# Three of eight k pairs of each gate/up block by Strassen's seven products

## The reference, cut to what matters

```
hn = rms_norm(h, ffn_norm[i])
h = h + (jax.nn.silu(hn @ w_gate[i]) * (hn @ w_up[i])) @ w_down[i]
```

## Time and profile before

| | us |
|---|---|
| median of 3 runs | 1336.36 (1336.12 to 1336.68) |
| profiled execution, its own time | 1335.7 |
| its span, first to last instruction | 1333.8 |
| PE busy in the span | 1327.3 (100%) |
| DVE busy | 789.4 (59%) |
| ACT busy | 629.2 (47%) |

### The profile page before, as it was taken

The page is one execution under the profiler, slowest core; times in us unless marked ns, Lnnn a source line. Parts: engine busy times, 40 slices in busy tenths (PEclk is TensorE's granted clock), DMA queues, the critical chain, the costliest instruction groups (busy, mean ns, idle before and its releaser), DMA issues.

```text
span 1333.8 us, 18088 instructions
## 1 busy us (share of the span) xinstructions
PE 1327.3 (100%) x6718; PEld 1097.8 (82%) x6718; DVE 789.4 (59%) x987; ACT 629.2 (47%) x796; POOL 54.2 (4%) x71
## 2 busy tenths in 40 slices
PE   9999999999999999999999999999999999999998
PEld 7788888887888888888888888888888888888887
DVE  6578885788585555555555554444555555555554
ACT  6576444543555545444444443344444444444543
POOL 4002000320000000000000000000000000000000
PEclk9999999999999999999999999999999999999999
DMA  8555544554445566666666666666666666655564
GB/s 270 172 182 164 152 143 135 158 155 136 136 128 156 176 190 189 190 194 185 188 188 194 186 189 196 196 190 192 186 189 192 189 186 190 189 188 190 189 191 141
DMA packets 126200, 238.34 MB, mean 179 GB/s; under 512 B 9711, under 2 KB 10786, under 8 KB 126138
## 3 DMA queue, kind: packets, MB, share of 16 engines
q1 hardware_dynamic: 126106, 237.48, 59.0%
q10 hardware_dynamic: 32, 0.01, 0.0%
HBM read 235.36 MB, written 2.10 MB: 178 GB/s over the span
## 4 chain that ended last, share of the span: by engine, by line
PE 99%; DMA 0%; DVE 0%; ACT 0%; issue 0%; ACTq 0%
PE pair L559 30%; PE pair L561 30%; PE pair L560 30%; PE bg L678 2%; PE bg L748 2%; PE bg L615 1%; PE bg L833 1%; PE bg L729 0%; PE bg L592 0%; PE pair L903 0%; PE pair L901 0%; PE pair L902 0%; PE bg L643 0%; PE bg L650 0%; PE bg L659 0%; DMA row_a<-in_attn_norm_dram 0%
## 5 line engine op out<-in xcount | busy, mean ns | idle before, releaser
L1233 DVE TENSOR_TENSOR w_lo<-raw,w_hi 128x1024 fp32r<-128x1024 f32 x442 | 540.3, 1225 | 420.4 <-ACT w_hi L919 417.5
L919 ACT ACTIVATE w_hi<-raw 128x1024 fp32r<-128x1024 f32 x442 | 467.8, 1061 | 485.0 <-PE pair L561 481.9
L559 PE MATMUL pair<-w_hi,xT_hi 128*128 128x512 f32 x1264 | 502.5, 398 | 0.5 <-DVE w_lo L1457 0.5
L561 PE MATMUL pair<-w_hi,xT_lo 128*128 128x512 f32 x1264 | 493.1, 390 | 0.0
L560 PE MATMUL pair<-w_lo,xT_hi 128*128 128x512 f32 x1264 | 492.5, 390 | 0.0
L561 PEld LDWEIGHTS pair<-w_hi,xT_lo 128*128 128x128 f32 x1264 | 237.2, 188 | 50.5
L559 PEld LDWEIGHTS pair<-w_hi,xT_hi 128*128 128x128 f32 x1264 | 237.4, 188 | 48.3 <-issue 0.7
L560 PEld LDWEIGHTS pair<-w_lo,xT_hi 128*128 128x128 f32 x1264 | 237.6, 188 | 46.0
L559 PE MATMUL pair<-w_hi,actT_hi 128*128 128x512 f32 x352 | 137.7, 391 | 0.0
L561 PE MATMUL pair<-w_hi,actT_lo 128*128 128x512 f32 x352 | 137.1, 389 | 0.0
L560 PE MATMUL pair<-w_lo,actT_hi 128*128 128x512 f32 x352 | 137.0, 389 | 0.0
(11 more groups left out here) (234 smaller groups left out, 875.4 us busy)
## 6 DMA issues: line engine op xcount, KB each, us to landing
raw<-in_w_in_dram SPq DMA_DIRECT2D x112, 512.0 KB, 3.8
raw<-in_w_gate_dram SPq DMA_DIRECT2D x88, 512.0 KB, 4.5
raw<-in_w_up_dram SPq DMA_DIRECT2D x88, 512.0 KB, 3.8
raw<-in_w_down_dram SPq DMA_DIRECT2D x88, 512.0 KB, 4.6
raw<-in_w_o_dram SPq DMA_DIRECT2D x32, 512.0 KB, 4.2
raw<-in_w_ple_gate_dram SPq DMA_DIRECT2D x32, 512.0 KB, 4.4
raw<-in_w_ple_proj_dram SPq DMA_DIRECT2D x4, 512.0 KB, 4.5
h<-in_x_dram SPq DMA_DIRECT2D x3, 512.0 KB, 7.7
```

What stands on the lines that cost most here:

```text
L559: mm(banks[t][:], hi[:, ts], wh, start=first, stop=False)
L561: m = mm(banks[t][:], lo[:, ts], wh, start=False, stop=last)
L919: f(w_hi[j % RING][:], raw[j % RING][:], ACT.Copy).then_inc(hi_ready, 1)
L1233: v.tensor_tensor(w_lo[j % RING][:], raw[j % RING][:], w_hi[j % RING][:].bitcast(F32), ALU.subtract).then_inc(lo_ready, 1)
```

## The change

In k pairs 3, 4 and 5 (`MIXED`) of every block, the gate unit and the up unit of the pair are used together. The pair's product is a 2 x 2 block product: tokens in two halves (0 and 1) by two k tiles (0 and 1), times two k tiles by (gate, up). It is made with Strassen's seven products (the Winograd form) instead of eight, 21 matmuls instead of 24.

- The differences of weights are made by DVE: t3, t1 (in place, over the up unit's first tile), t2 and t4, each from the one before or from raw tiles; ACT rounds them, DVE makes their low parts (`split_mixed`). Their buffers `t_hi`, `t_lo` are single and are free when PE has used them (`t_used`).
- The sums and differences of activations (`F_raw`, `F_hi`, `F_lo`) are made once, in steps hA 3, 4 and 5. For the other five pairs (`PLAIN`) hA also makes the difference of the two token halves (`d_hi`, `d_lo`), since the second up bank now gathers a product with this difference.
- The units come in the order `SEQ`: gate 0, 1, 2, 6; gate and up 3; gate 7; gate and up 4; up 0; gate and up 5; up 1, 2, 6, 7.
- The pair products go to `bg[0]`, `bg[1]`, `bg[2]` and the four `pair` banks. Sums bring them together: four on DVE for the gate after the third pair (`MIXED_END`), with one copy on ACT, and three for up at the end of the block.
- PE turns `act_s` behind unit 2 instead of unit 3, and waits for `ff_free` before the first mixed pair. Steps hA 6 and 7 come one unit earlier. SP's fetch into a mixed gate unit's tile waits for `t4_ready`.

```diff
-            at[U_WO + (n + 1) * UPB + 2][g].append(("hA", 2 * n + g))
+            at[U_WO + (n + 1) * UPB + (2 if n < 3 else 1)][g].append(("hA", 2 * n + g))
...
+MIXED = (3, 4, 5)
+PLAIN = [g for g in range(UPB) if g not in MIXED]
+SEQ = ([("gate", g) for g in PLAIN[:4]] + [("gate", MIXED[0]), ("up", MIXED[0])] + [("gate", g) for g in PLAIN[4:]]
+       + [("gate", MIXED[1]), ("up", MIXED[1])] + [("up", PLAIN[0])]
+       + [("gate", MIXED[2]), ("up", MIXED[2])] + [("up", g) for g in PLAIN[1:]])
+MIXED_END = SEQ.index(("up", MIXED[-1]))
...
+                        if j >= RING and SEQ[j - RING] in [("gate", m) for m in MIXED]:
+                            sp.wait_ge(t4_ready, i * len(MIXED) + (len(MIXED) * at + MIXED.index(SEQ[j - RING][1]) + 1))
+                            fetch(j, w, KU * g, i * CB + at * CB)
+                        else:
+                            load(i * (2 * UPB) + (u0 + j), j, w, KU * g, i * CB + at * CB)
...
+            def product(o, hi, lo, wh, wl, first, last):
+                mm(o, hi, wh, start=first, stop=False)
+                mm(o, hi, wl, start=False, stop=False)
+                return mm(o, lo, wh, start=False, stop=last)
+            def mixed_units(u, j, q, n):
...
+                use(u)
+                product(bg[0][:], xT_hi[:, k0, a0], xT_lo[:, k0, a0], gh[:, 0, :], gl[:, 0, :], first, last)
+                product(pair[0][0][:], xT_hi[:, k1, a0], xT_lo[:, k1, a0], gh[:, 1, :], gl[:, 1, :], False,
+                        last).then_inc(unit_used, 1)
+                use(u + 1)
+                product(pair[1][1][:], xT_hi[:, k0, a1], xT_lo[:, k0, a1], uh[:, 0, :], ul[:, 0, :], first, False)
+                product(pair[1][0][:], F_hi[:, q, 1, :], F_lo[:, q, 1, :], uh[:, 1, :], ul[:, 1, :], first,
+                        False).then_inc(unit_used, 1)
+                pe.wait_ge(t3_lo_ready, n)
+                product(bg[2][:], F_hi[:, q, 2, :], F_lo[:, q, 2, :], t_hi[:, 2, :], t_lo[:, 2, :], first, last)
+                pe.wait_ge(t24_lo_ready, n)
+                product(bg[1][:], F_hi[:, q, 0, :], F_lo[:, q, 0, :], t_hi[:, 0, :], t_lo[:, 0, :], first, last)
+                product(pair[0][1][:], xT_hi[:, k1, a1], xT_lo[:, k1, a1], t_hi[:, 1, :], t_lo[:, 1, :], False,
+                        last).then_inc(t_used, 1)
...
+                        if q == 0:
+                            pe.wait_ge(pair_free[1], i * 2 + b0)
+                            if not peeled:
+                                for n in range(2):
+                                    pe.wait_ge(ff_free[n], i + n0)
+                        mixed_units(u, j, q, i * len(MIXED) + (len(MIXED) * n0 + q + 1))
...
-                    if j == 3 and not peeled:
+                    if j == 2 and not peeled:
                         pe.wait_ge(pair_free[1], i * 2 + b0)
+                        pe.wait_ge(gate_sum, i * 2 + 2 * n0)
                         turn_act()
...
+            def split_mixed(u, j, n, n0_first):
+                act.wait_ge(t3_ready, n)
+                if not n0_first:
+                    act.wait_ge(t_used, n - 1)
+                f(t_hi[:, 2, :], t3_raw[:], ACT.Copy).then_inc(t3_hi_ready, 1)
+                act.wait_ge(t1_ready, n)
+                act.wait_ge(unit_used, u - (RING - 1))
+                f(w_hi[j % RING][:], raw[j % RING][:], ACT.Copy).then_inc(hi_ready, 1)
+                act.wait_ge(t4_ready, n)
+                f(t_hi[:, 0:2, :], t24_raw[:], ACT.Copy).then_inc(t24_hi_ready, 1)
...
+            def split_mixed(u, j, n, first):
+                jg, ju = (j - 1) % RING, j % RING
...
+                v.tensor_tensor(t3_raw[:], raw[ju][:, 1, :], raw[ju][:, 0, :], ALU.subtract).then_inc(t3_ready, 1)
+                dve.wait_ge(t3_ready, n)
+                v.tensor_tensor(raw[ju][:, 0, :], raw[ju][:, 0, :], raw[jg][:, 0, :], ALU.subtract).then_inc(t1_ready, 1)
+                dve.wait_ge(t1_ready, n)
+                v.tensor_tensor(t24_raw[:, 0, :], raw[ju][:, 1, :], raw[ju][:, 0, :], ALU.subtract).then_inc(t2_ready, 1)
+                dve.wait_ge(t2_ready, n)
+                v.tensor_tensor(t24_raw[:, 1, :], raw[jg][:, 1, :], t24_raw[:, 0, :], ALU.subtract).then_inc(t4_ready, 1)
+                split(u, j)
+                dve.wait_ge(t3_hi_ready, n)
+                v.tensor_tensor(t_lo[:, 2, :], t3_raw[:], t_hi[:, 2, :].bitcast(F32), ALU.subtract).then_inc(t3_lo_ready, 1)
+                dve.wait_ge(t24_hi_ready, n)
+                v.tensor_tensor(t_lo[:, 0:2, :], t24_raw[:], t_hi[:, 0:2, :].bitcast(F32),
+                                ALU.subtract).then_inc(t24_lo_ready, 1)
...
+                    if j == MIXED_END:
+                        p1 = act_s[1]
+                        dve.wait_ge(p1_copied, i + (n0 + 1))
+                        v.tensor_tensor(v_s[:], bg[1][:], p1[:], ALU.add).then_inc(v_ready, 1)
+                        v.tensor_tensor(gate_s[0][:], pair[0][0][:], p1[:], ALU.add).then_inc(gate_sum, 1)
+                        dve.wait_ge(v_ready, i * 2 + (2 * n0 + 1))
+                        v.tensor_tensor(u_s[:], bg[2][:], v_s[:], ALU.add).then_inc(v_ready, 1)
+                        dve.wait_ge(v_ready, i * 2 + (2 * n0 + 2))
+                        v.tensor_tensor(gate_s[1][:], pair[0][1][:], u_s[:], ALU.add).then_inc(gate_sum, 1)
...
+                        v.tensor_tensor(v_s[:], pair[1][1][:], v_s[:], ALU.add).then_inc(up_sum, 1)
+                        v.tensor_tensor(u_s[:], pair[1][1][:], u_s[:], ALU.add).then_inc(up_sum, 1)
+                        dve.wait_ge(up_sum, i * 3 + (3 * n0 + 1))
+                        v.tensor_tensor(v_s[:], pair[1][0][:], v_s[:], ALU.add).then_inc(up_sum, 1)
```

More of the change, by code:

```diff
@@ L251, in build @@
         ident = sb("ident", [P, P])
+        triu_at = place[0]
+        t24_raw = sb("t24_raw", [P, 2, CB], at=triu_at)
         triu = sb("triu", [P, P])
@@ L259, in build @@
         NROW = 3 * KT + 3
+        assert triu_at + 4 * KIB <= place[0]
         rows = sb("rows", [NROW - KT, P])
@@ new lines, in mixed_units @@
+            def mixed_units(u, j, q, n):
+                first, last = q == 0, q == len(MIXED) - 1
+                g, a0, a1 = MIXED[q], slice(0, P), slice(P, TOK)
+                k0, k1 = KU * g, KU * g + 1
+                gh, gl = w_hi[j % RING], w_lo[j % RING]
+                uh, ul = w_hi[(j + 1) % RING], w_lo[(j + 1) % RING]
+                use(u)
[12 more added lines that the diff above has]
+                        last).then_inc(t_used, 1)
@@ new lines, in gate_up @@
+            def gate_up(i, u0, b0, n0, peeled):
+                for j, (side, g) in enumerate(SEQ):
+                    u = i * (2 * UPB) + (u0 + j)
+                    if g in MIXED:
+                        if side == "up":
+                            continue
+                        q = MIXED.index(g)
+                        if q == 0:
[4 more added lines that the diff above has]
+                        mixed_units(u, j, q, i * len(MIXED) + (len(MIXED) * n0 + q + 1))
+                        continue
+                    use(u)
+                    if j == 0:
+                        pe.wait_ge(pair_free[0], i * 2 + b0)
+                    if peeled and n0 == 0 and g in (PLAIN[0], 6) and side == "gate":
+                        for n in (range(6) if g == PLAIN[0] else (6, 7)):
+                            wait_read(pe, ("hA", n))
+                    for kk in range(KU):
+                        k = KU * g + kk
+                        wh, wl = w_hi[j % RING][:, kk, :], w_lo[j % RING][:, kk, :]
+                        if side == "gate":
+                            last = k_tile(j, kk, xT_hi[:, k, :], xT_lo[:, k, :], pair[0], k == 0, False)
+                        else:
+                            d = KU * PLAIN.index(g) + kk
+                            product(pair[1][1][:], xT_hi[:, k, P:TOK], xT_lo[:, k, P:TOK], wh, wl, False, k == KT - 1)
+                            last = product(pair[1][0][:], d_hi[:, d, :], d_lo[:, d, :], wh, wl, False, k == KT - 1)
@@ L947, in post @@
                         act.wait_ge(x1_full, 1)
+                    if step == "hA" and b in MIXED:
+                        if b - 1 in MIXED:
+                            wait_read(act, (step, b - 1))
+                        for kk in range(2):
+                            k = 2 * b + kk
+                            f(xg[:, kk, :], bk[:, kk * TOK:(kk + 1) * TOK], ACT.Copy,
+                              scale=gains[:, col + k:col + k + 1]).then_inc(xg_ready, 1)
+                        q = MIXED.index(b)
+                        act.wait_ge(xg_ready, 2 * (q + 1))
+                        f(xT_hi[:, 2 * b, 0:P], xg[:, 0, 0:P], ACT.Copy)
+                        f(xT_hi[:, 2 * b + 1, :], xg[:, 1, :], ACT.Copy).then_inc(x_hi, 2)
+                        act.wait_ge(form_ready, 4 * q + 1)
+                        f(xT_hi[:, 2 * b, P:TOK], F_raw[:, 0, :], ACT.Copy)
+                        act.wait_ge(form_ready, 4 * (q + 1))
```

(45 more changed lines are left out.)

89 lines of the change are left out of this document (67 added, 22 removed).

## The result

| | us |
|---|---|
| before, median of 6 runs | 1336.43 |
| changed kernel, median of 6 runs | 1343.95 (1341.92 to 1347.19) |
| ratio, 95% interval | 1.0057 (1.0044 to 1.0070) |
| profiled execution's span | 1341.3 (before 1333.8) |
| mean granted clock in it | 0.995 (before 0.999) |

The kernel is slower by 0.6%, 7.5 us, though PE got 99 matmuls fewer. The runs spread over 5 us where those of before spread over 0.6.

A forecast was written before the change was run, and what follows sets the result against it. PE was taken to bound the kernel, busy all the time with 99% of the chain. Saved matmuls -22.4, waits for the turned banks +21.3 and the first block +2.75 gave +1.65 us: 1338.0 us, range 1331.5 to 1346.

The forecast's parts named there:

- the three signs: Whole kernel: chances of 0.24 for faster by over 0.2%, 0.35 for within 0.2%, 0.41 for slower.
- its own band: Whole kernel: 1334 to 1343 us, from a wait of 2.1 to 2.8 us per block; chance 0.52.
- further waits in each block: Behind `turned`, margins of 0.3 to 0.5 us fail: 0.6 us per block in ten blocks, 1344 us; chance 0.20.
- 99 matmuls at 0.2267: -22.4: Mixed pairs on PE: 99 fewer matmuls at 0.2267 us each save 22.4 us, 2.04 per block.
- The wait for the turned banks, nine times 2.37: Before the first mixed pair, PE waits for DVE to free the turned banks: nine blocks, 21.3 us.
- T+13.91: DVE's `turned` operations end 13.91 us after T, the first matmul of a block; PE wants them at T+11.76.
- The first block: 2.75: First gate/up block: PE loses 1.55 us at unit 3 for hA, some 0.6 at each later pair.
- The rest of the block at nothing: Behind the first pair's wait, thin cover suffices: 0 us taken, bounds 0 to 1 us per block.
- The clock: Behind PE's idle times, the clock falls to 1.2 GHz, half a us nine times: +4.5, 1342.6 us; chance 0.05.
- The rival that own waits cost nothing: In DVE's chain, waits on its own results are free, shortening each PE wait to 1.89 us: 1332.2; chance 0.12.
- The rival that DVE keeps ahead: At the turned banks, DVE frees them in time, leaving only the first block's 2.75 us loss: 1316.7; chance 0.11.

The follow-up runs named there:

- own_bank: Changed kernel with the pairs' first product in the unused bank bg[3] and the ff_free wait moved before the product into bg[1]: 1316.17 us, ratio 0.9852.
- bank_low3: Changed kernel with the first product in bg[3], plus one unused 128x512 DVE operation in each pair of the loops' blocks: 1324.29 us, ratio 0.9911.
- turned_inside: Changed kernel with `turned` called inside the first pair's `split_mixed`, ahead of the lows of t, same banks: 1316.15 us, ratio 0.9850.
- turned_j2: Changed kernel with `turned` one split earlier, ahead of unit 6, same banks: 1329.04 us, ratio 0.9947.
- before_gap_long: Kernel before, PE waiting behind its turn for both turned banks, plus one unused DVE operation in `turned`: 1365.59 us, ratio 1.0224.
- before_gap: Kernel before, without mixed products, PE waiting right behind its turn until both turned banks are free, in the loops' nine blocks: 1364.38 us, ratio 1.0213.
- bank_ha0: Changed kernel with the first product in bg[3], and hA 6 and 7 in unit 0 of the first gate/up block instead of unit 1: 1316.23 us, ratio 0.9850.
- low_twice: Changed kernel with one more unused 128x512 DVE operation ahead of `turned` in each block of the loops: 1352.37 us, ratio 1.0125.

## Why the prediction was right, and what it missed

The time lies in the range, and slower was the likeliest of the three signs, at 0.41. Part of that is luck. The forecast itself was 1338.0, no measurable change, and its own band ended at 1343; 1343.95 lies above that, and inside the range only because the range was stretched to 1346 for a rival, further waits in each block, that did not occur. By its steps, against the medians:

- **99 matmuls at 0.2267: -22.4.** Right. With the wait gone the block is 42.41 instead of 44.43 long, 2.02 less, against 2.04.
- **The wait for the turned banks, nine times 2.37.** The mechanism, its place and its count were right; the size is 2.53, 22.8 us in all. I counted the DVE chain to end at T+13.91; in the trace above, with the first sum standing for T+0.29, it ends at T+13.98. The rest is PE's restart, 0.26 beyond the idle time where I had 0.22, and the next matmuls, which start 0.23 apart instead of 0.227.
- **The first block: 2.75.** Nearly right. own_bank's trace has idle times of 1.38, 0.17 and 0.27 there, and with the slower start behind each PE is held up by 1.6, 0.4 and 0.5, where I had 1.55, 0.6 and 0.6. By the medians own_bank stands 20.2 under before, of 22.4, so 2.2 is lost in all; that takes in every other small difference between the two kernels.
- **The rest of the block at nothing.** Right: own_bank has no wait there. The margin was larger than I wrote (bank_low3). DVE's busy time was overstated: 40.3 us in a block of 44.94 and not 42.4, since I added durations of 0.69 that overlap where starts are 0.61 apart. The chain was counted by starts and doesn't suffer from it.
- **The clock.** This is the step that failed. I gave a fall 0.05 and half a us each, because no row showed PE idle for 2 us; but then no row spoke against it either. It costs 1.6 us each time, and the profiled execution has three: 4.8 us. That the rival's own total, nine times half a us, comes near this is luck: three longer falls stand against nine short ones. The falls are also what spreads the runs: those with a clock of 0.997 and 0.993 took 1341.9 and 1347.2, an estimated two and five falls over the 1339 us without any.

Sum: -22.4 + 22.8 + 2.2 + 4.8 = 7.4, against 7.5 measured. Three falls for the median are an estimate from the one trace. Without the falls it would be 1339.0 (own_bank's 1316.2 and nine waits of 2.53), and the forecast was 1338.0.

- **The rival that own waits cost nothing:** in DVE's timeline above, the differences, each of which waits for its predecessor's result, start 0.72 to 0.73 apart, and the first two sums, which don't, 0.61. That rival is out. The trace disagrees with the Trainium skill here ("VectorE: DVE Perf Modes", section "The DRAIN you can't avoid", a semaphore costs nothing extra) for an operation that waits on its predecessor's semaphore, as it did in the earlier trace rows.
- **The rival that DVE keeps ahead** fell in the changed kernel, but only by a place in the queue: turned_inside is that case, and 1316.15 is what I had for it (1316.7).

What is open: what decides in which blocks the clock falls. It fell behind idle times of 2.0 to 2.9 us (the lists' totals over nine) in some blocks and in none behind 1.1 (turned_j2), nor behind the single 1.4 in own_bank's first block; but the 2.5 us gaps of before_gap_long brought fewer falls in their trace than the 2.0 us ones of before_gap, three against four. The experiments varied only the gap's length and whether mixed products are in the kernel. The Trainium skill's page "TensorE: Matmul & The Clock Gate", section "Part 1: The HAM clock gate", has the clock at one of two rates, by how active PE has been; the trace agrees with the two rates (intervals of 0.427 and 0.227).

Five of the versions are faster than both kernels. The fastest three, turned_inside with 1316.15, own_bank with 1316.17 and bank_ha0 with 1316.23 us, are the same within the spread, 1.5% under the kernel before.

## What to carry to other kernels

When an engine that was half idle gets filled, ask for each buffer that it frees who waits for it and how many operations now stand ahead of the freeing; the average share says nothing of this, and here moving one call ahead of three operations was worth 27.8 us. A saving on the bounding engine is real only if no wait opens on it, and an idle time of about 2 us there can cost its clock as well: put a price on that if the trace has no such gap to look at.

## What the runs showed of the hardware

- After PE had stood idle for 2.0 to 3.1 us among dense matmuls, the granted clock in some blocks went to half (15 times behind 36 such waits, in the traces of the changed kernel, low_twice and the two before_gap ones). The slow matmuls began between 0 and 1.9 us after PE had resumed (1.3 in the trace above, 0 in before_gap's at 1063.91) and went on for some 3 to 4 us (3.35 above). One such fall made a block 1.4 to 1.6 us longer. It came with and without the mixed products.
- After a wait PE's loss is 0.24 to 0.28 us more than the idle time in the row, behind a wait of 0.17 as behind one of 2.25 (own_bank's first block and the changed kernel).
- On DVE a 128x512 operation that waits for its predecessor's own result starts 0.72 to 0.73 us after it, one that doesn't 0.61 (the changed kernel, 681.31 to 689.71).
